# Two transformer blocks on one core: the queries, keys and values go first, and three groups of products move in between the attention's items

## The reference, cut to what matters

```python
h = rms_norm(x, norm1_g)
q, k, v, bg, cg, xc = split(h @ w_in)              # 1024 columns each
y_attn = chunked_relpos_attention(q, k, v, ...)    # 16 heads of 64, bias by distance, softmax
y_conv = bg * conv3(cg * xc)                       # causal, per channel
gates = sigmoid(h @ w_gate + b_gate)               # g_attn, g_conv
merged = g_attn * (y_attn @ w_attn_proj) + g_conv * (y_conv @ w_conv_proj)
x = x + merged @ w_out
x = x + square(relu(rms_norm(x) @ w_up)) @ w_down
```

## Time and profile before

| | |
|---|---|
| median of 3 runs | 2930.36 us (2926.49 to 2931.91) |
| the profiled execution | 2931.76 us |
| its span in the profile | 2930.0 us |
| PE busy | 2313.1 us (79%) |
| DVE busy | 1826.2 us (62%) |
| ACT busy | 632.2 us (22%) |
| POOL busy | 790.1 us (27%) |
| HBM read | 790.23 MB, 272 GB/s over the span |

### The profile page before, as it was taken

How to read it: one execution, slowest core, us unless ns; L and a number is a source line. 1 busy time by engine, 2 the same in 40 slices (tenths; PEclk the granted TensorE clock), 3 DMA queues, 4 the chain that set the end, 5 groups by cost and what they waited for, 6 DMA issues and landing times. The chain is left out here.

```text
span 2930.0 us, 26186 instructions
## 1 busy us (share of the span) xinstructions
PE 2313.1 (79%) x9012; PEld 1706.8 (58%) x9012; DVE 1826.2 (62%) x3679; ACT 632.2 (22%) x1424; POOL 790.1 (27%) x544
## 2 busy tenths in 40 slices
PE   8999999999889999899899779987534455555454
PEld 7887588887668888666788666766411122122111
DVE  1101335413245897765777784857888888888886
ACT  1001502101431301245121024711111111111110
POOL 0000000000000244321443431312266555546552
PEclk9999599999979999999999888979768777777777
DMA  4433137753223799962899964725499999999996
GB/s 174 153 145 121 24 131 285 274 187 129 72 85 132 281 390 411 361 236 83 365 422 421 416 254 157 268 84 231 173 398 421 405 422 421 421 396 421 421 421 284
DMA packets 114659, 798.24 MB, mean 272 GB/s; under 512 B 13280, under 2 KB 16480, under 8 KB 19040
## 3 DMA queue, kind: packets, MB, share of 16 engines
q0 software_dynamic: 74880, 541.10, 45.4%
q1 hardware_dynamic: 39648, 255.47, 23.2%
HBM read 790.23 MB, written 6.29 MB: 272 GB/s over the span
## 5 line engine op out<-in xcount | busy, mean ns | idle before, releaser
L482 PE MATMUL PS<-reg,ring 128*128 128x256 f32 x6016 | 1364.2, 388 | 38.3 <-DVE reg L1273 13.5
L482 PEld LDWEIGHTS PS<-reg,ring 128*128 128x128 f32 x6016 | 1157.0, 194 | 226.3 <-issue 50.0
L433 POOL DMA_INDIRECT uv<-in_expert_uv,experts x322 | 527.2, 1637 | 1958.2 <-DVE experts L1168 946.3
L1210 DVE SCALAR_TENSOR_TENSOR acc<-uv,coef,acc 128x1024 f32<-128x1024 f32 x261 | 335.3, 1285 | 10.0 <-DVE coef L1195 0.8
L461 PE MATMUL PS<-uv,diag 128*128 128x512 f32 x228 | 154.0, 826 | 237.3 <-ACT diag L852 237.3
L1183 DVE CUSTOM_DVE_ANT_0 uv<-uv,h_tok 128x1024 f32<-128x1024 f32 x226 | 269.3, 1219 | 53.8 <-DMA uv<-in_expert_uv,experts 53.7
L461 PEld LDWEIGHTS PS<-uv,diag 128*128 128x128 f32 x228 | 59.0, 274 | 335.8 <-issue 335.8
L859 ACT ACTIVATE acts<-dots 128x2 f32<-128x2 f32 (+1 forms) x192 | 39.1, 204 | 993.4 <-DVE dots L1183 899.3
L461 PE MATMUL PS<-reg,diag 128*128 128x512 f32 x228 | 163.7, 874 | 106.0 <-ACT diag L852 106.0
L461 PEld LDWEIGHTS PS<-reg,diag 128*128 128x128 f32 x228 | 60.8, 281 | 207.2 <-issue 207.2
L433 POOL DMA_INDIRECT reg<-in_expert_uv,experts x114 | 141.9, 1245 | 88.7 <-PE PS L461 61.9
(11 more groups left out here) (241 smaller groups left out, 2354.1 us busy)
## 6 DMA issues: line engine op xcount, KB each, us to landing
ring<-in_weights SPq DMA_DIRECT2D x228, 1024.0 KB, 6.8
uv<-in_expert_uv,experts POOLq DMA_INDIRECT x322, 14.1
reg<-in_x_t SPq DMA_DIRECT2D x2, 1024.0 KB, 5.8
kv_half<-reg SPq DMA_DIRECT2D x1, 2048.0 KB, 11.0
reg<-in_sub_t SPq DMA_DIRECT2D x2, 1024.0 KB, 4.7
x_tokens<-reg SPq DMA_DIRECT2D x2, 1024.0 KB, 4.0
toep<-in_rel_pad SPq DMA_DIRECT2D x16, 128.0 KB, 3.2
reg<-kv_half SPq DMA_DIRECT2D x1, 2048.0 KB, 15.0
```

The costliest lines, as they stand in the source:

```text
L433: gp.indirect_dma_start(UV[r], None, a["expert_uv_2"], bass.IndirectOffsetOnAxis(ap=experts[:, e % 256:e % 256 + 1], axis=0))\
L482: mm = pe.matmul(out_tile(n, t), w[:, t * P:(t + 1) * P], mv, start=first and k == 0, stop=last and k == KT - 1)
L1210: dve.scalar_tensor_tensor(acc[:, :], v, c, acc[:, :], ALU.mult, ALU.add).then_inc(acc_done, 1)
```

## The change

The order of blocks in each half becomes Q1, K1, V1, CG, XC, BG, and then GC, CP, GA (`FILL1`), AP, WO. The 12 blocks of `FILL1`, 192 matmuls, are no longer a stretch of their own: `weights_block(..., single=True)` yields after each matmul, and PE's `attention` takes three of them ahead of the scores of an item and three behind its transposes, six an item. `filled(i)` lists the tiles that were finished in item i-1; ACT and DVE evacuate these at item i (`fill_tile`), and run the expert steps of their blocks there. These tiles have lanes 4 and 5, PSUM banks 6 and 7. The attention makes do with six banks instead of eight: scores three instead of four, values one instead of two. The transposes of item i-1 stand where those of item i stood, and the values of a head come two items later. PE waits for all evacuations of BG ahead of the attention. The bias tables of heads 2 to 15 are loaded between the blocks of `FILL1` and AP. Since Q1 0 is now the first block of a half, the tables of heads 0 and 1, with the wait for `corner`, stand ahead of it in SP's order.

```diff
-    _run = plain_run(CG, XC, BG, GC, GA, CP, Q1, K1, V1, AP_, WO)
+    _run = plain_run(Q1, K1, V1, CG, XC, BG, GC, CP, GA, AP_, WO)
...
+FILL1 = (GC, CP, GA)
+N_ITEMS = NH1 * TT
+PER_ITEM = 4 * len(FILL1) * 2 * KT // N_ITEMS
+
+def filled(i):
+    return [j for j in range(8 * len(FILL1)) if (KT * (j + 1) - 1) // PER_ITEM == i - 1]
...
-TICKS = [int(hf == 1 and (kind, i) not in ((V1, 3), (WO, 3), (DN, 15), (V2, 0), (V2, 1), (WO2, 3))) for hf, kind, i in SEQ]
+TICKS = [int(hf == 1 and (kind, i) not in ((BG, 3), (WO, 3), (DN, 15), (V2, 0), (V2, 1), (WO2, 3))) for hf, kind, i in SEQ]
...
                 if (kind, i) == (Q1, 0):
                     toeplitz(hf, 0)
                     toeplitz(hf, 1)
+                    next_head = 2
                 if (kind, i) == (WO, 0):
-                    for h in range(2, NH1):
-                        toeplitz(hf, h)
+                    assert next_head == NH1
+                if kind in FILL1 or kind == AP_:
+                    f = n - NO[hf, FILL1[0], 0]
+                    while next_head < NH1 and (TT * next_head - 5) * PER_ITEM <= (f - 3) * 2 * KT:
+                        toeplitz(hf, next_head)
+                        next_head += 1
...
+                for i in range(4):
+                    for t in range(2):
+                        evac_wait(pe, NO[hf, BG, i], t)
                 pe.wait_ge(hn_done, 32 * hf + 16)
```

In PE's attention:

```diff
-                for i in range(n_items):
-                    if i + 3 < n_items:
-                        scores(i + 3)
-                    transposes(i)
-                    if i and i % TT == 0:
-                        values(i // TT - 1)
+                for i in range(N_ITEMS):
+                    if i >= 4 and i % TT == 0:
+                        values(i // TT - 2)
+                    for _ in range(PER_ITEM // 2):
+                        next(fill)
+                    if i + 3 < N_ITEMS:
+                        scores(i + 3)
+                    if i:
+                        transposes(i - 1)
+                    for _ in range(PER_ITEM // 2):
+                        next(fill)
+                transposes(N_ITEMS - 1)
+                values(NH1 - 2)
                 values(NH1 - 1)
```

In ACT's attention:

```diff
+                def fill_tile(j):
+                    kind, i, t = FILL1[j // 8], j % 8 // 2, j % 2
+                    n = NO[hf, kind, i]
+                    if kind != CP:
+                        tile_wait(act, n, t)
+                        dst, b = (GCM, 8) if kind == GC else (GA_[hf], 0)
+                        act.activation(dst[:, j % 8, :], out_tile(n, t), ACT.Tanh, bias=half_b[:, b + j % 8:b + j % 8 + 1],
+                                       scale=0.5).then_inc(evac_sem(n, t), 1)
+                    if t:
+                        tick(hf, kind, i)
...
+                for i in range(N_ITEMS + 1):
+                    for j in filled(i):
+                        fill_tile(j)
+                    if i + 1 < N_ITEMS:
                         exps(i + 1)
+                    if i < N_ITEMS:
+                        normalise(i)
+                    if i >= 2:
+                        prob_copy(i - 2)
+                prob_copy(N_ITEMS - 1)
```

In DVE's attention:

```diff
+                for i in range(N_ITEMS + 1):
+                    if i < N_ITEMS:
+                        inverse(i)
+                    for j in filled(i):
+                        fill_tile(j)
+                    if i + 2 < N_ITEMS:
                         biased(i + 2)
+                    if i % 4 == 3 and i >= 7:
+                        y_copy((i - 7) // 4)
+                    for j in filled(i):
+                        if j % 2:
+                            tick(hf, FILL1[j // 8], j % 8 // 2)
                 y_copy(7)
```

More of the change, by code:

```diff
@@ L78 @@
 for _n in range(NB):
-    if evacuates(_n) and SEQ[_n][1] in (VM, OM):
+    if evacuates(_n) and SEQ[_n][1] in (VM, OM) + FILL1:
         _lanes = (4, 5)
@@ L466, in _, with weights_block @@
             experts_pe = expert_steps()
-            def weights_block(n, moving, token_major=False, first=True, last=True, fresh=None):
+            def weights_block(n, moving, token_major=False, first=True, last=True, fresh=None, single=False):
                 pe.wait_ge(w_loaded[n % NRING], 16 * (n // NRING + 1))
@@ L483, in weights_block @@
                                            start=first and k == 0, stop=last and k == KT - 1)
+                        if single and k < KT - 1:
+                            yield t
                     mm.then_inc(tile_done, 1)
@@ L568, in values @@
                     pe.wait_ge(p_copy, base + TT * (hd + 1))
-                    if pair >= 2 and hd % 2 == 0:
-                        pe.wait_ge(y_done, 8 * hf + pair - 1)
+                    if pair and hd % 2 == 0:
+                        pe.wait_ge(y_done, 8 * hf + pair)
                     for kt in range(2 * hf + 2):
@@ L577, in values, with fill_products @@
                     mm.then_inc(pv_mm, 1)
-                n_items = NH1 * TT
+                def fill_products():
+                    for kind, moving in ((GC, h), (CP, lambda k: YC[hf][:, k, :]), (GA, h)):
+                        for i in range(4):
+                            yield from weights_block(NO[hf, kind, i], moving, single=True)
+                fill = fill_products()
                 for i in range(3):
                     scores(i)
-                for i in range(n_items):
-                    if i + 3 < n_items:
-                        scores(i + 3)
-                    transposes(i)
-                    if i and i % TT == 0:
-                        values(i // TT - 1)
+                for i in range(N_ITEMS):
[4 more added lines that the diff above has]
+                    if i + 3 < N_ITEMS:
+                        scores(i + 3)
+                    if i:
+                        transposes(i - 1)
+                    for _ in range(PER_ITEM // 2):
+                        next(fill)
+                assert next(fill, None) is None
+                transposes(N_ITEMS - 1)
+                values(NH1 - 2)
                 values(NH1 - 1)
@@ L695, in half @@
             def half(hf):
[L696 to L700, removed]
-                for i in range(4):
[L702 to L708, removed]
+                for i in range(4):
+                    for t in weights_block(NO[hf, Q1, i], h, fresh=4 * hf * KT if i == 0 else None):
+                        if hf and 2 * i + t == 1:
+                            pe.wait_ge(tok_copy, 10)
                         if 2 * i + t:
@@ L1311, in y_copy, with fill_tile @@
                     dve.wait_ge(pv_mm, NH1 * hf + 2 * pair + 2)
-                    dve.tensor_copy(Q[:, pair, :], PS[:, 6 + pair % 2, 0:T]).then_inc(y_done, 1)
-                n_items = NH1 * TT
+                    dve.tensor_copy(Q[:, pair, :], PS[:, 5, 0:T]).then_inc(y_done, 1)
+                def fill_tile(j):
+                    kind, i, t = FILL1[j // 8], j % 8 // 2, j % 2
+                    n = NO[hf, kind, i]
+                    if kind == CP:
+                        tile_wait(dve, n, t)
+                        evac_wait(dve, NO[hf, GC, i], t)
+                        dve.scalar_tensor_tensor(GCM[:, j % 8, :], GCM[:, j % 8, :], 1.0, out_tile(n, t),
+                                                 ALU.add, ALU.mult).then_inc(evac_sem(n, t), 1)
                 biased(0)
                 biased(1)
-                for i in range(n_items):
-                    if i + 2 < n_items:
-                        biased(i + 2)
-                    inverse(i)
-                    if i % 4 == 2 and i >= 6:
-                        y_copy(i // 4 - 1)
+                for i in range(N_ITEMS + 1):
[4 more added lines that the diff above has]
+                    if i + 2 < N_ITEMS:
+                        biased(i + 2)
+                    if i % 4 == 3 and i >= 7:
[3 more added lines that the diff above has]
+                            tick(hf, FILL1[j // 8], j % 8 // 2)
                 y_copy(7)
@@ L1328, in half @@
                     dve.memset(toep[0:64, b, 0:64], NEG).then_inc(corner, 1)
+                only_ticks(hf, Q1)
+                for which, kind, tiles, gain in ((0, K1, Q, "q_g"), (1, V1, K[hf], "k_g")):
+                    for i in range(4):
+                        if i == 1:
+                            head_inverse(hf, which)
+                        for j in (2 * i, 2 * i + 1):
+                            if 3 <= j < 7:
+                                head_scale(hf, which, 2 * j - 6, tiles[:, 2 * j - 6, :], col(gain))
+                                head_scale(hf, which, 2 * j - 5, tiles[:, 2 * j - 5, :], col(gain))
+                        tick(hf, kind, i)
                 if hf == 0:
@@ L1366, in half @@
                         tile_wait(dve, n, t)
-                        dve.tensor_tensor(YC[:, j, :], out_tile(n, t), c, ALU.mult).then_inc(evac_sem(n, t), 1)
```

(1 more changed line is left out.)

42 lines of the change are left out of this document (17 added, 25 removed).

## The result

The changed kernel takes 2969.9 us (median of 4 runs), the kernel before 2930.3 beside it: a ratio of 1.0139, interval 1.0127 to 1.0151, 39.6 us slower. The forecast was 2950, 20 us slower, in a range of 2921 to 2981. So the direction and the places are right, and the size is half of what came. The profiled execution has a span of 2968.0 us against 2930.0, 38.0 more.

The account below looks back on a forecast made before the run. PE, busy nearly throughout until about 2100 us, was taken as the bound. First-half merge -29, second half +29 and late starts +20 gave +20 on 2930.4, so 2950 us; range 2921 to 2981.

Parts of the forecast that it names:

- late starts, with their clock: Start of each half: first weights queued behind tables and `corner`, PE 10 and 8.2 us late, clock 1.8; +20 us.
- first half, merge: First half's attention with its 12 blocks: full clock instead of 1.2 GHz, 127.2 us against 156.4; -29 us.
- second half, work at full clock in the merged stretch: Second half's attention with products: 75 of attention, 83.0 of products, 7.2 of change-overs; 165 us of PE work.
- its stalls and tail: Second half's merged stretch: PE waits for copies behind twelve expert steps, 31 us, and a tail of 4 us.
- its low clock: Second half's merged stretch: four stalls and the tail lower the clock, 1.7 us each; 8.5 us.
- second half, the stretch before: Second half ahead of attention: 271.2 us, 2 of remaining waits, 10 uncovered while DVE finishes BG's evacuations.
- (b): Rival: the start costs nothing, the first weights not being held up; 2930 us, no change; chance 0.05.
- (a): Rival: expert steps are hidden, stalling PE under half a microsecond in the merged stretch; 2912 us; chance 0.15.
- (c): Rival: a step costs two more waits between ACT and DVE, 2.7 us each step, 30 us; 2980 us; chance 0.10.
- (d): Rival: the clock stays at 1.2 GHz through the second half's merged stretch; half the doubling gives 3030 us; chance 0.04.
- The rule on table loads: Trainium skill's drain of 1.38 us beside each load: 22 loads of 11 steps would add up to 30 us.

Follow-up runs that it names:

- e1: The changed kernel with the bias tables of heads 0 and 1 behind a half's first four weight loads instead of ahead of them: 2946.8 us.
- e4: The changed kernel with the merge in the first half only; the second half runs GC, CP, GA as plain products behind BG: 2923.0 us.
- e2: The changed kernel with ACT's part of an expert step at the end of the item, behind `prob_copy`, instead of ahead of exps: 2920.1 us.
- e6: The changed kernel with e2 and e3 together, the step behind the copy and CG, XC, BG ahead of Q1, K1, V1: 2894.9 us.
- e9: The changed kernel with the experts' gelu replaced by a tanh, which needs no table load behind an exp; the experts' output differs: 2928.3 us.
- e3: The changed kernel with CG, XC, BG ahead of Q1, K1, V1; the tables stay ahead of Q1, no longer the first block: 2944.5 us.
- e5: The changed kernel with e1 and e2 together, tables behind the first weight loads and the expert step behind the copy: 2898.4 us.
- e7: The changed kernel with e1 and e4 together, tables behind the first weight loads and the merge in the first half only: 2895.3 us.

## Why the forecast was right in its places and too small

The terms of the sum, against what the profile of the change shows:

| term | forecast | measured |
|---|---|---|
| late starts, with their clock | +20 | +21.4 |
| first half, merge | -29 | -30.8 |
| second half, work at full clock in the merged stretch | 165 | 160.2 |
| its stalls and tail | 31 + 4 | 41.2 |
| its low clock | 8.5 | 19.2 |
| second half, the stretch before | 283.2 | 287.9 |
| rest | 0 | +1.6 |

*Late starts.* The first product comes at 27.41, forecast 27.2. From AP to the second start it takes 636.75 us instead of 628.71, 8.0 more; as AP no longer begins at the low clock (1.6), the start itself is 9.6 late, forecast 8.2. The clock behind it cost 1.6, forecast 1.8. Here the first weights are issued at 973.80 and used at 979.95, 6.15 us, between the 4.0 and 6.8 of the earlier trace rows, where 4.6 was taken. e1 shows the cause and the size by taking it away. That the first start came so near is partly luck: `corner` was set at 18.5 us, 1.5 earlier than the 20.0 of the sum, and the first weights took 6.49 us from issue to use (20.92 to 27.41), 1.9 more than the 4.6. Rival (b) is out.

*First half.* 125.6 us against 127.2, at a granted clock of 1.00 by the window of the stretch, and the 1.6 in AP as said. e4 shows it by itself: 8.4 us faster than the kernel before with the 21.4 of the late starts in it, so about 30.

*Work in the second half.* Two items of a head with their products repeat at 10.01 us (1218.84 to 1228.85), 160.2 for 16; the 0.22 taken for a change-over was too much.

*Stalls.* The mechanism is the one forecast, and e2 shows it: the step stands in front of the copy, and moving it behind gives 49.8 us back. The rows of single stalls: items 3, 11 and 27 cost 6.06, 6.40 and 6.72 us (forecast 5.0 to 5.9), item 19 7.06 (6.9), item 16 2.99 (2.8), 6 and 8 1.79 and 1.67 (1.0 and 3.0), the tail 3.06 (4). The others, even items without routing, were put at 0.4 and took 1.46, 1.46, 1.55 and 0.92. The sum is 6.2 too low, over half of it in these four.

*Low clock: the term that failed.* The forecast put it at 8.5 us, and it measured 19.2. It was counted for four long stalls and the tail, 1.7 each, as the earlier trace rows had shown for 8.81 us of idle time, and put at nothing for everything shorter. Measured, by the same instructions at the two levels: the four long stalls cost 2.9, 2.1, 1.7 and 2.3 beyond themselves, 8.9; the tail 1.5. Nearly that much was forecast. Not forecast were the first scores behind the wait for BG (5.59 us, where e6 takes 3.17: 2.4), and the short stalls. From the transposes to the next item's scores 4.90 us pass at the full clock; behind the stalls of 1.79, 1.67, 2.99 and 1.55 us it was 6.5 each time, 1.6 more; behind the two of 1.46, nothing and 0.2. Together 6.7. The sum of all is 19.5, and the stretch less work and stalls leaves 19.2. e2 and e9 agree from the other side: with stalls of 7.4 and 22.3 us, what is left over work and stalls is 4.7 and 7.3.

The length of a stall does not settle its price. PE's windows from the transposes to the next scores (PE's busy time, granted clock, DMA share, GB/s), in the change behind 1.79 and 1.46 us:

```profile
1235.80:1242.33 6.53, 6.53 (x24) 0.74 0.54 134
1290.88:1295.78 4.90, 4.90 (x24) 1.00 0.57 140
```

In e1 behind 2.40 us, and in e3 behind the same 2.40:

```profile
1225.96:1230.85 4.89, 4.89 (x23) 1.00 0.31 62
```

```profile
1220.96:1228.79 7.83, 7.83 (x23) 0.61 0.12 38
```

The stall of 1.79 us cost nothing in e1, a stall of 1.46 cost 1.6 in e3, and one of 1.55 nothing there. In all, what is left over work and stalls in the merged stretch is 14.9 us in e1 and 17.2 in e3, each with stalls of 42.7. So a part of the 19.2 belongs to this one profiled execution, and what decides the price of a short stall stays open; that it is nothing, as the forecast had it, is refuted.

*The stretch before the second half's attention.* It is 206.5 us (979.95 to 1186.48) and the 83.0 moved, less the 1.6 of clock counted above. Waits were 4.1 instead of 2, five blocks ran 1.7 us longer (36.46 against 34.77) at the lower clock, and the wait for BG was 10.9, not 10. e1, e3 and e4 say more about this wait than the forecast did: it moves (12.06, then 8.88 before a head mean, then 11.72 for GA), and no order of the blocks removed it.

*Rivals.* (a), hidden steps, is what e2 makes of the kernel, not what the change does. (c), 30 us for two more waits a step, came nearest in size (2980), but its mechanism is not there: from the dot products to the end of the copy ACT takes 4.7 us, where the sum had 4.75. (d) is out, the stretch is granted 0.89.

The rule on table loads: e9 took the loads away and gained 30.8 us in the stretch, close to the 30 that the drain of 1.38 us would have added in the forecast's terms. But this is no sign of the drain. ACT's rows above show gelu 0.02 us behind its load and the next load 0.02 us behind gelu. Of the 30.8 us 18.9 came off the stalls, and the rest off the clock. Two loads of 1.28 for each of 12 steps are 30.8 us too, but that agreement is chance: taking them away shortened the stalls by 18.9 only. The "~1380 ns DRAIN" of the Trainium skill (ScalarE: Activation LUTs, "What ACT_TABLE_LOAD costs") does not show beside the loads of these rows, while its 1283 ns for the load do (mean 1283 in the row).

What stays open: why the lag at the end of BG keeps its length in every order; what decides whether a short stall lowers the clock; where the 11 us of e9 behind AP come from; and whether the 3 us between e5, e6 and e7 are real.

## What to carry to other kernels

Work that fills the gaps of one engine has bookkeeping on the others: put it behind the operation that the filled engine waits for next, not ahead. Here that was a move of three lines and worth 50 us. When a block becomes the first of its phase, all that is queued with it becomes first too: read the DMA queue's order again. And merge only where the gaps are, for the half whose clock was low gained 31 us, and the other, already nearly full, gained nothing measurable and took on twelve stalls.

## What was not expected of the hardware

Short idle times can cost clock as well. In the change, four stalls of 1.55 to 2.99 us between stretches of full work were each followed by 1.6 us lost at the 1.2 GHz level, two of 1.46 us by 0 and 0.2. In e1 the stalls of 1.79 and 2.40 us were followed by the full clock, in e3 that of 2.40 by 2.9 us lost: the same idle time, at the same place of the program, has no fixed price. In the chain of stalls of the change the clock added 17 us to 41.

PE's windows in the change behind the stall of 6.06 us, where the granted clock is 0.58, and then 1.00:

```profile
1212.00:1220.00 8.00, 7.18 (x19) 0.58 0.11 47
1220.00:1225.00 5.00, 5.00 (x27) 1.00 0.38 102
```

The first megabyte of weights at the second start took 6.15 us from issue to use, with four small transfers ahead of it and three of its size issued behind it, longer than the 4.0 of the quiet transfers in the earlier trace rows.
